# Weighing with the two heads of a pair in the two column halves of the array, and softmax inverses multiplied in late

## The reference, cut to what matters

```python
# mixer A: 8 heads, chunks of 64 queries, 576 keys each
sc = einsum('bqhd,bkhd->bhqk', qc, kc) * scale + bias
p = softmax(where(valid, sc, NEG_INF), axis=-1)
out = einsum('bhqk,bkhd->bqhd', p, vc)
# mixer B: 8 query heads on 2 key heads, 128 keys, a learned sink
m = maximum(max(sc, axis=-1), sink)
p = exp(sc - m)
p = p / (sum(p, axis=-1) + exp(sink - m))
o = einsum('bnhgqk,bnkhd->bnqhgd', p, vb)
```

## Time and profile before

| | |
|---|---|
| median of three runs | 2673.0 us |
| the profiled execution | 2678.14 us, span 2676.2 us, mean granted clock 0.996 |
| PE busy | 2631.9 us, 12920 multiplies |
| DVE, ACT, POOL busy | 1923.2, 1159.0, 252.6 us |
| attention of layer 0, layer 1 | 281.8 to 515.6 us, 1603.6 to 1835.9 us |

### The profile page before, as it was taken

One profiled execution on the slowest core, in us unless ns is written; L12 is line 12 of the kernel. 1 busy time (PEld: TensorE's weight loads), 2 busy tenths in 40 slices (PEclk: granted clock), 3 DMA queues, 4 the chain that ended last, 5 costly groups with the idle time before them and its releaser, 6 DMA issues. The chain is left out here.

```text
span 2676.2 us, 36725 instructions
## 1 busy us (share of the span) xinstructions
PE 2631.9 (98%) x12920; PEld 2208.2 (83%) x12920; DVE 1923.2 (72%) x3579; ACT 1159.0 (43%) x2429; POOL 252.6 (9%) x390
## 2 busy tenths in 40 slices
PE   8999999999999999999999999999999999999998
PEld 6888888888888888888878888888888888888886
DVE  8766667644787787767996666775448887776687
ACT  6222677732533333344542227775325333333444
POOL 0000311244100000000000011112440000000000
PEclk9999999999999999999999999999999999999999
DMA  4323433253222332385423243332531332234843
GB/s 147 122 104 115 155 102 111 75 183 115 87 99 103 114 118 84 106 269 176 153 99 122 99 144 123 119 97 88 188 120 61 114 110 88 103 114 136 267 124 126
DMA packets 185236, 333.21 MB, mean 125 GB/s; under 512 B 17248, under 2 KB 62688, under 8 KB 185056
## 3 DMA queue, kind: packets, MB, share of 16 engines
q1 hardware_dynamic: 176832, 307.67, 34.6%
q10 hardware_dynamic: 8224, 23.20, 2.6%
HBM read 237.09 MB, written 92.80 MB: 123 GB/s over the span
## 5 line engine op out<-in xcount | busy, mean ns | idle before, releaser
L1203 PE MATMUL ps<-op_hi,up_hi 128*128 128x512 f32 x1232 | 479.9, 390 | 2.5 <-DVE third_sum L2781 2.5
L1205 PE MATMUL ps<-op_hi,up_lo 128*128 128x512 f32 x1232 | 479.3, 389 | 0.0
L1204 PE MATMUL ps<-op_lo,up_hi 128*128 128x512 f32 x1232 | 479.3, 389 | 0.0
L1203 PE MATMUL ps<-in_hi,up_hi 128*128 128x512 f32 x728 | 286.9, 394 | 3.3 <-DVE up_lo L2279 2.1
L1205 PE MATMUL ps<-in_hi,up_lo 128*128 128x512 f32 x728 | 285.0, 392 | 0.0
L1204 PE MATMUL ps<-in_lo,up_hi 128*128 128x512 f32 x728 | 285.0, 392 | 0.0
L1878 ACT ACTIVATE up_hi<-up_raw 128x512 fp32r<-128x512 f32 x252 | 158.0, 630 | 276.9 <-PE ps L1205 271.1
L1203 PEld LDWEIGHTS ps<-op_hi,up_hi 128*128 128x128 f32 x1232 | 231.3, 188 | 51.1 <-issue 3.3
L1205 PEld LDWEIGHTS ps<-op_hi,up_lo 128*128 128x128 f32 x1232 | 231.3, 188 | 48.3
L1204 PEld LDWEIGHTS ps<-op_lo,up_hi 128*128 128x128 f32 x1232 | 231.3, 188 | 47.6
L1173 POOL CAST w_hi<-w_raw 128x256 fp32r<-128x256 f32 x192 | 85.3, 486 | 1757.7 <-DMA w_raw<-w_lin 1199.7
(11 more groups left out here) (266 smaller groups left out, 5406.8 us busy)
## 6 DMA issues: line engine op xcount, KB each, us to landing
up_raw<-w_gu SPq DMA_DIRECT2D x42, 1024.0 KB, 5.1
act_raw<-ff_saved SPq DMA_DIRECT2D x154, 256.0 KB, 2.7
w_quarter<-w_lin SPq DMA_DIRECT2D x52, 512.0 KB, 4.4
w_raw<-w_lin SPq DMA_DIRECT2D x48, 512.0 KB, 3.7
ff_saved<-ff_block SPq DMA_DIRECT2D x88, 256.0 KB, 2.0
ff_saved<-ff_mix SPq DMA_DIRECT2D x66, 256.0 KB, 2.1
gated<-gates_saved SPq DMA_DIRECT2D x32, 512.0 KB, 4.1
stage<-in_saved SPq DMA_DIRECT2D x48, 256.0 KB, 2.8
```

The source lines that it names most:

```text
L1203: pe.matmul(out, w1, x1, start=first, stop=False, skip_group_check=True)
L1204: pe.matmul(out, w1, x0, start=False, stop=False, skip_group_check=True)
L1205: return pe.matmul(out, w0, x1, start=False, stop=last, skip_group_check=True)
```

## The change

- `weigh` handles a pair of heads at once. The stationary operand is now a block of values, 128 keys x 64 columns of head e; the turned probabilities of that head are moving, 128 columns; the result of head e goes to partitions 64e to 64e + 63 of `o_ps`, features on partitions. Blocks are the outer loop, heads the inner one.
- A's pairs are weighed one by one (an odd unit u at step u + 3). In B the pairs with even p are weighed at u + 5, in the same step as the next pair (odd p, u + 3): four units in one run. B's two units of a pair are also turned together, into 256 columns of `t_ps`, and moved by one ACT copy; `probs_t` has three buffers in A, two in B.
- DVE copies the unscaled pair from `o_ps` straight into `x_sb`. `o_tok`, `turn_pair` and `take_pair` are gone.
- The row sums of eight units are inverted in one go, in B after one sink exponential and one sum for all eight; PE turns the 128x8 inverses into 8x128, DVE copies them out, SP saves them to DRAM and reads them back as rows spread over partitions, a quarter (four units) at a time: `inverse_rows` is [128, 256]. DVE multiplies it into `x_sb` in place (`scale_heads`). Steps from the first unit of an eight: turned 10, saved 11, spread 12 and 16, scaled 15 and 19.
- `split_o` waits for the scaled heads: for all but the last phase before its first tile, for all before its seventh.
- The gate fill has another order with the same sum in each phase; at the start of a phase one step of it is put ahead of the scores. All logits but a layer's last now use one buffer (before: two in turn).
- `vb_odd` is in two pieces, so that three DMAs fill its first half.

```diff
-FILL_A = ((3, 3, 3, 2, 2, 2, 2, 1, 1, 1, 1, 1, 1, 1, 1, 1), (1, 1, 1, 1, 1, 0, 1, 0, 1, 0, 0, 0, 1, 0, 0, 0))
+FILL_A = ((3, 3, 3, 3, 2, 3, 1, 2, 1, 1, 0, 1, 1, 1, 0, 1), (1, 1, 0, 1, 0, 1, 0, 1, 0, 1, 0, 1, 0, 1, 0, 0))
...
+def weighed_at(u):
+    mixer, _, _, p = unit(u)
+    return u + (5 if mixer == "B" and p % 2 == 0 else 3)
...
+TURNED_AT, SAVED_AT, SPREAD_AT, SCALED_AT = 10, 11, (12, 16), (15, 19)
...
+            def save_inverse(L, eight):
+                n = L * EIGHTS + eight
+                sp.wait_ge(inverse_step, 2 * n + 2)
+                sp.dma_start(inverse_dram[n], inverse_turned[0:EIGHT, :]).then_inc(inverse_saved, 16)
...
+            def spread_inverse(L, quarter):
+                n = L * QUARTERS + quarter
+                sp.wait_ge(inverse_saved, 16 * (n // 2 + 1))
+                if n > 0:
+                    sp.wait_ge(head_scaled, n)
+                for e in range(2):
+                    src = inverse_dram[n // 2][QUARTER * (n % 2):QUARTER * (n % 2 + 1), :].rearrange("(p e) n -> e p n", e=2)
+                    sp.dma_start(inverse_rows[e * HD:(e + 1) * HD, :].rearrange("d (p n) -> d p n", p=2),
+                                 src[e:e + 1].to_broadcast([HD, 2, P])).then_inc(inverse_spread, 16)
...
             def weigh(L, u):
...
                 for j in range(nb):
-                    mm = pe.matmul(o_ps(u)[:, e * HD:(e + 1) * HD], probs_t[u % 2][:, j * P:(j + 1) * P], values[j],
-                                   start=(j == 0), stop=(j == nb - 1))
+                    for e in range(2):
+                        rows = slice(e * HD, (e + 1) * HD)
+                        mm = pe.matmul(o_ps(u)[rows, :], blocks[j][:, rows], turns[e][:, j * P:(j + 1) * P],
+                                       start=(j == 0), stop=(j == nb - 1))
                 mm.then_inc(head_done, 1)
-            def turn_pair(L, u):
...
+            def turn_inverse(L, s, eight):
+                pe.wait_ge(inverse_step, 2 * (L * EIGHTS + eight) + 1)
...
+                pe.transpose(i_ps, inverse[:, stats_of(eight)], ident[:, :]).then_inc(inverse_turned_done, 1)
...
             def take_turned(L, u):
-                cols = key_blocks(mixer, p) * P
+                cols = key_blocks(mixer, p) * P if mixer == "A" else 2 * P
...
             def take_heads(L, u):
-                dve.tensor_tensor(o_tok[:, n % 2, :].rearrange("p (e d) -> p e d", e=2),
-                                  o_ps(u).rearrange("p (e d) -> p e d", e=2), inverse, ALU.mult).then_inc(head_free, 1)
+                src = o_ps(u) if mixer == "A" else o_ps(u).rearrange("p (h n) -> p h n", h=2)
+                dve.tensor_copy(x_of(u), src).then_inc(head_free, 1)
+            def scale_heads(L, quarter):
...
+                dve.wait_ge(inverse_spread, 32 * (n + 1))
+                if mixer == "A":
+                    x = x_sb[:, g, p * P:(p + 2) * P]
+                    dve.tensor_tensor(x, x, inverse_rows[:, :], ALU.mult).then_inc(head_scaled, 1)
```

More of the change, by code:

```diff
@@ L557, in o_ps, with x_of, stat_of, stats_of @@
             return bank(5 if mixer == "B" and u // 2 % 2 else 6)[:, 0:P]
+        def x_of(u):
+            mixer, g, _, p = unit(u)
+            if mixer == "A":
+                return x_sb[:, g, p * P:(p + 1) * P]
+            tile, chunk = GROUPS + g // 2 * 2, chunk_of(g, p)
+            return x_sb[:, tile:tile + 2, chunk * CHUNK:(chunk + 1) * CHUNK]
+        def stat_of(u):
+            return slice(u % NSTAT, u % NSTAT + 1)
+        def stats_of(eight):
+            first = EIGHT * eight % NSTAT
+            return slice(first, first + EIGHT)
+        i_ps = bank(7)[0:EIGHT, 2 * P:3 * P]
+        def turned_to(u):
+            mixer, _, _, _ = unit(u)
+            return probs_t[u % NTURNED if mixer == "A" else u // 2 % 2]
+        def odd_values(block):
+            return vb_odd[0][:, block, :] if block < ODD_FIRST else vb_odd[1][:, block - ODD_FIRST, :]
+        def logit_of(i):
+            return logit[1 if i == GATE_HALVES - 1 else 0][:, :]
+        def soft(u):
+            mixer, _, _, _ = unit(u)
+            first = u // NPROBS % 2 * P if mixer == "B" else 0
+            return probs[u % NPROBS][:, first:first + (P if mixer == "B" else A_COLS)]
+        def soft_last(u):
+            mixer, _, _, _ = unit(u)
+            return u - (2 * NPROBS if mixer == "B" and u % PHASE >= NPROBS else NPROBS)
         v_ps = bank(7)[:, 0:2 * P]
@@ L1360, in weigh @@
                     chunk = chunk_of(g, p)
-                    v, block = (vb, chunk // 2) if chunk % 2 or chunk == 0 else (vb_odd, chunk // 2 - 1)
-                    values = [v[:, block, e * HD:(e + 1) * HD]]
-                    if e == 0 and p == 0:
+                    blocks = [vb[:, chunk // 2, :] if chunk % 2 or chunk == 0 else odd_values(chunk // 2 - 1)]
+                    turns = [turned_to(u)[:, e * P:(e + 1) * P] for e in range(2)]
+                    if p == 0:
                         pe.wait_ge(v_ready, L * VALUES + V_PARTS * (rank(CONV.index(("vb", 0, min(g, 1)))) + 1))
-                    if e == 0 and (g, p) in ((0, 2), (1, 0)):
-                        pe.wait_ge(vb_shifted[g], 32 * (L + 1))
@@ L1770, in attention @@
+                if u >= NTURNED:
+                    if u % PHASE < NTURNED + 1:
+                        weighed = u // 2
+                    elif mixer == "A":
+                        weighed = (u - NTURNED) // 2 + 1
+                    else:
+                        weighed = u // 2 - 1
+                    act.wait_ge(head_done, L * HEAD_PAIRS + weighed)
+                act.activation(turned_to(u)[:, 0:cols], t_ps[:, 0:cols], ACT.Copy).then_inc(turned_ready, 1)
             def attention(L):
@@ L1772, in attention @@
                     raise_half(L, c)
[L1773 to L1776 removed]
+                for s in range(UNITS + 2):
                     for c, part in turns_at(s - 1):
                         take_values(L, c, part)
[L1779 removed]
+                    if 2 <= s < UNITS + 2 and (unit(s - 2)[0] == "A" or s % 2 == 1):
                         take_turned(L, s - 2)
@@ L1782, in attention @@
                         soften(L, s)
+                    if eight_at(s, EIGHT) is not None and unit(s - 1)[0] == "B":
+                        soften_sinks(L, eight_at(s, EIGHT))
                     for e in range(2):
```

286 lines of the change are left out of this document (172 added, 114 removed).

## The result

The changed kernel takes 2684.5 us (median of six runs, 2680.2 to 2688.2) against 2673.0 for the kernel before (six runs, 2670.0 to 2677.1): a ratio of 1.004, interval 1.0028 to 1.0052. The forecast was 2639. The profiled execution has a span of 2684.1 us for 2676.2.

The account below looks back on a forecast made before the run. PE, busy 98% of the span at nearly full clock, was taken to bound the kernel. Terms -68.1 + 38.4 - 14.3 + 3.6 + 10 - 4 = -34.4 us gave 2639 against 2673.0; range 2600 to 2694.

Parts of the forecast that it names:

- Weighing, -68.1: 1216 load-and-multiply records of values and probabilities on PE: slot falls from 0.112 to 0.056 us, column halves side by side, -68.1 us.
- Rival 1: Column halves of the weighing don't overlap while switches between full-array and half-array products cost as forecast: +18.8 us, 2692; chance 0.15.
- Changes of form, +38.4: PE passing between full-array and half-array products around weighing runs: 192 times at 0.2 us, +38.4 us.
- Pair transposes, -14.3: PE's 128 transposes of finished head pairs go, at 0.112 us each: -14.3 us.
- Inverse transposes, +3.6: PE's 32 new transposes of inverted row sums, 16 a layer, at 0.112 us each: +3.6 us.
- The round through DRAM, 0: Saving inverses to DRAM and spreading them back for DVE's scaling in the attention: hidden, 0 us.
- Rival 3: Round through DRAM late in B, holding up DVE's scaling and SP's stage loads: +26 us, 2665; chance 0.14 together with rival 4.
- rival 4: Halves overlap, but each switch between full and half array costs 0.27 us and ACT's waits 20: 2663; chance 0.14 with rival 3.
- ACT's waits, +10: PE waiting in the attention until ACT has taken the last turned probabilities: 1.2 us a phase, 8 phases, +10 us.
- B's holes, -4: PE's idle time in B's first phases, 3.3 and 3.0 us, of which 4 us were taken back.
- The tail, 0: End of a layer's attention: last scaled quarters are needed only behind 48 gate products and first branch products, 0 us.

Follow-up runs that it names:

- run without the round: Changed kernel without saving and spreading the inverses through DRAM, rows of ones multiplied in instead: 2668.0 us, 0.9981 of the kernel before.
- the thinned weighing: Kernel with later spread and shorter tail (2668.2 us), 832 of A's 960 weighing products left out: 2647.4 us, 0.9903 of the kernel before.
- loads first: Changed kernel with SP's saves and spreads of the inverses moved behind the loads of the same step: 2688.8 us, 1.0057 of the kernel before.
- both a step later: Changed kernel with spreads at steps 13 and 17 and scalings at 16 and 20: 2671.2 us, 0.9994 of the kernel before.
- scaling alone later: Changed kernel with scalings at steps 16 and 20, spreads still at 12 and 16: 2703.9 us, 1.0114 of the kernel before.
- round on POOL: Changed kernel with saves and spreads of the inverses issued from POOL's queue instead of SP's: 2715.9 us, 1.0158 of the kernel before.
- the weight load moved: Changed kernel with each gate weight tile loaded 5 steps after the last-but-one tile's start, for 4: 2684.1 us, 1.0045 of the kernel before.

## Why the prediction was wrong, step by step

The attention was to fall by 34.4 us and rose by 7.5, 42 off. By its terms:

- **Weighing, -68.1: right.** 1216 x (0.112 - 0.054) = -70.5. Rival 1 is out. The Trainium skill (TensorE: Matmul & The Clock Gate, "Measured speedup vs the span model") has no row for two column tiles; by my estimate from its 2.38x for three it would have been 1.59x. The trace shows 0.109 to 0.054, all of 2x.
- **Changes of form, +38.4: a little too dear.** 192 x 0.173 = +33 (0.15 going in, 0.20 coming out). The Trainium skill (TensorEngine Tiling (Array Packing), "Key Properties") says that a change drains the engine; the trace agrees as far as it goes, with this gap at each change.
- **Pair transposes, -14.3: right.** They are gone. **Inverse transposes, +3.6: too cheap.** The 32 are there, and PE idles 9.5 us ahead of them, by the group shown above. I had costed the record and not its wait: it shares a PSUM bank with the turned values and needs DVE's reciprocal. +13, of which 3 lie behind the last scores of a layer (1.75 and 1.31 us of waiting) and 10 in the attention.
- **The round through DRAM, 0: wrong.** I checked that its data would be in time, not whom its waits hold. Its price is 16.5 us. Rival 3 had both halves of the mechanism, late rows and SP in front of the stage loads, and put it at 26, on top of a gain that didn't come; I had given it, with rival 4, a chance of 0.14.
- **The clock: missing from the sum.** +8.5 us a layer, 17 in all. The earlier trace rows had shown full clock, and I took it for granted. It is not a loss beside the round's: 13.8 of the 17 lie in the four A phases that ran at full clock without the round. By the estimate of half the slow stretch it turned holes of 1.6, 2.6 and 1.9 us into losses of 3.3, 6.0 and 5.3.
- **ACT's waits, +10, and B's holes, -4: far too small a loss.** What is left of the 7.5 is 7.5 + 70.5 - 33 + 14.3 - 10 - 17 = 32 us, for 6. The run without the round leaves the same: its attention is 8.0 us shorter than before, its only slow phase costs 1.6, and -8.0 + 70.5 - 33 + 14.3 - 10 - 1.6 = 32. So this second loss is not the round's. I compared the sums of busy time (83% and 87%) and called neither a bound. But with one score buffer and one `t_ps` the engines take turns: in a five-block step DVE's row maximum of 0.82 + 0.08 and ACT's copy of 0.70 must fit into PE's other work between two scores or two turns. PE's work in an A phase shrank by about 15%, and its cover with it. That PE's own slots don't set these steps alone is shown by the thinned weighing; how the 32 us split between DVE's and ACT's chains isn't settled, since taking one away let the other grow. The 32 are a remainder and hold the errors of the terms above: PE's idle time in the rows of the attention grew by 22 us, from 12 to 34, and short waits hide in the durations of its records. Of B's holes, the idle time in the first B phases fell only from 3.3 and 3.0 to 2.5 and 2.2, 1.7 for the 4.
- **The tail, 0:** 1.8 to 1.9 us a layer behind the last scores. Most of it is PE's wait for the last inverses, counted above. DVE's last two scalings wait 3.4 us each for their rows with the split behind them, but of that only four waits of about 0.16 us for `o_lo` reach PE in layer 0, and three in layer 1.

The steps that failed, and turned the direction, are the waits: the round's 0, and PE's waits for ACT and DVE at 6. Each has an experiment, but for the second it shows that there is a wait, not whose it is.

The 16.5 us in one table, waits over the span of the profiled execution beside the median time:

| kernel | queue for the scaling before | ACT for stage loads | DVE for rows | us |
|---|---|---|---|---|
| before | - | 22.7 | - | 2673.0 |
| after | 106.4 | 33.5 | 15.2 | 2684.5 |
| loads first | 61.3 | 23.3 | 24.5 | 2688.8 |
| both a step later | 91.7 | 26.3 | 17.7 | 2671.2 |
| scaling alone later | 170.6 | 43.8 | 18.2 | 2703.9 |
| round on POOL | 171.4 (POOL) | 21.4 | 48.0 | 2715.9 |
| no round | - | 20.3 | - | 2668.0 |

Late stage loads and late rows are two edges of one timing: loads first lengthened the waits for rows, scaling alone later those for stage loads, and a step of slack for both is what helps. Of DVE's waits for rows, up to 14 us lie in the two tails, so the columns aren't a sum, and an engine's wait costs only what reaches PE. How much of the 16.5 is slow clock is estimated above, not measured: the mean clock was 0.994 to 0.997 in the runs without the round, for 0.990 to 0.994 with it and 0.995 to 0.998 before. The wide spread of the runs with the weight load moved suggests that one small hole more or less decides.

## What to carry to other kernels

When PE's work in a pipelined stage shrinks, compare not busy shares but, step by step, each hand-over between engines with the work that PE has left between asking and needing; with single buffers there the gain is lost before any engine looks full. A new DMA on a shared in-order queue costs what its wait holds back, not what it moves: list what is queued behind each of its semaphores, on whichever queue it goes. Look behind each new hole of PE at the granted clock: a slow stretch that follows it can cost more than the hole.

## What the runs showed of the hardware

- Two products on different column halves, 64 columns loaded and 128 streamed in plain float32, run at a slot of 0.054 us when they alternate, 0.092 on average when heads are the outer loop, and 0.109 between two on the same half.
- Passing from full-array to half-array products costs 0.15 us, passing back 0.20, on top of the slots.
- In the changed kernel the granted clock was at half (1.2 GHz) for 3.4 or 6.8 us after PE had idled 1.6 to 2.6 us. After 1.60 us in the kernel before, and after 1.28 us with the weight load moved, it stayed at full. One kernel's runs differ by 15 us with the mean clock between 0.989 and 0.996.
- A spread row load (64 KB from 1 KB read again and again) takes 0.62 us of its queue to issue and 2.6 to land.
